# The first pair of seven products prepared during the output projection, and the product that sums the squares placed behind a low pass

## The reference

```python
mixed = jnp.concatenate([o_a, o_b, o_c], axis=-1)   # three attention groups
h = h + mixed @ w_out                               # output projection, 1024 x 1024
f = rms_norm(h, ffn_norm)
gate, up = jnp.split(f @ w_gate_up, 2, axis=-1)     # 1024 x (2 x 2816)
return h + (jax.nn.silu(gate) * up) @ w_down        # 2816 x 1024
```

## Time and profile before

| | us |
|---|---|
| median of three runs | 1295.46 |
| the profiled execution, its own time | 1295.57 |
| its span | 1293.5 |
| PE busy | 1259.0 (97%) |
| DVE busy | 901.5 (70%) |
| ACT busy | 633.9 (49%) |
| POOL busy | 439.4 (34%) |

### The profile page before, as it was taken

How to read it: one execution, slowest core, us unless ns; L and a number is a source line. 1 busy time by engine, 2 the same in 40 slices (tenths; PEclk the granted TensorE clock), 3 DMA queues, 4 the chain that set the end, 5 groups by cost and what they waited for, 6 DMA issues and landing times.

```text
span 1293.5 us, 22962 instructions
## 1 busy us (share of the span) xinstructions
PE 1259.0 (97%) x9174; PEld 1187.0 (92%) x9174; DVE 901.5 (70%) x1520; ACT 633.9 (49%) x1016; POOL 439.4 (34%) x230
## 2 busy tenths in 40 slices
PE   7999999998999999899999999999989999999998
PEld 7989999998999999899998889988779999997887
DVE  4598898488888888722236999984888888885110
ACT  5575556655444444522235665385464445454221
POOL 2563322143222222244445453122432222214543
PEclk9999999999999999999999999999999999999999
DMA  5312211033222231222223221110322332212333
GB/s 189 94 56 83 66 34 34 34 104 115 108 99 99 99 102 63 99 98 98 97 93 101 73 77 55 50 34 24 123 98 98 112 118 99 99 66 98 99 111 115
DMA packets 27440, 113.58 MB, mean 88 GB/s; under 512 B 3664, under 2 KB 4304, under 8 KB 21968
## 3 DMA queue, kind: packets, MB, share of 16 engines
q1 hardware_dynamic: 26624, 111.18, 25.2%
q10 hardware_dynamic: 720, 1.09, 0.2%
HBM read 108.79 MB, written 2.10 MB: 86 GB/s over the span
## 4 chain that ended last, share of the span: by engine, by line
PE 84%; DVE 9%; ACT 3%; issue 2%; DMA 1%; POOL 1%; SPq 0%; DVEq 0%; ACTq 0%; POOLq 0%
PE ps L1243 21%; PE ps L857 17%; PE ps L1249 11%; PE ps L863 8%; PE ps L954 5%; PE ps L960 5%; PE ps L955 5%; PE ps L1084 2%; PE ps L1057 1%; PE ps L1067 1%; PE ps L1032 1%; DVE rstd L2041 1%; DVE score L1866 1%; DMA raw<-in_groups 1%; PE ps L1141 1%
## 5 line engine op out<-in xcount | busy, mean ns | idle before, releaser
L724 POOL TENSOR_TENSOR wlo<-raw,whi 128x1024 fp32r<-128x1024 f32 x116 | 282.9, 2440 | 477.1 <-ACT whi L1327 476.6
L1327 ACT ACTIVATE whi<-raw 128x1024 fp32r<-128x1024 f32 x116 | 122.4, 1057 | 223.8 <-PE ps L863 179.1
L954 PE MATMUL ps<-xhi,whi 128*128 128x264 f32 (+1 forms) x632 | 177.6, 310 | 0.0
L955 PE MATMUL ps<-xlo,whi 128*128 128x264 f32 (+1 forms) x632 | 171.4, 300 | 0.0
L857 PE MATMUL ps<-hhi,whi 128*128 128x264 f32 (+1 forms) x528 | 159.0, 323 | 5.2 <-DVE hlo L2105 5.2
L857 PE MATMUL ps<-hlo,whi 128*128 128x264 f32 (+1 forms) x528 | 159.0, 323 | 0.0
L954 PEld LDWEIGHTS ps<-xhi,whi 128*128 128x128 f32 x632 | 119.1, 189 | 4.5 <-issue 0.4
L955 PEld LDWEIGHTS ps<-xlo,whi 128*128 128x128 f32 x632 | 119.2, 189 | 3.9
L857 PEld LDWEIGHTS ps<-hhi,whi 128*128 128x128 f32 x528 | 100.4, 190 | 13.5 <-DVE hlo L2105 5.8
L857 PEld LDWEIGHTS ps<-hlo,whi 128*128 128x128 f32 x528 | 100.2, 190 | 7.8
L829 POOL TENSOR_TENSOR sums_a<-raw 128x1024 f32<-128x1024 f32 x22 | 53.9, 2449 | 151.4 <-PE ps L1249 151.4
(11 more groups left out here) (275 smaller groups left out, 3337.8 us busy)
## 6 DMA issues: line engine op xcount, KB each, us to landing
raw<-in_weights SPq DMA_DIRECT2D x116, 512.0 KB, 3.3
raw<-in_groups SPq DMA_DIRECT2D x42, 1024.0 KB, 4.8
out_hT<-h SPq DMA_DIRECT2D x7, 256.0 KB, 4.5
h<-in_hT SPq DMA_DIRECT2D x4, 264.0 KB, 6.5
h<-in_hT ACTq DMA_DIRECT2D x4, 264.0 KB, 6.1
cst<-in_consts SPq DMA_DIRECT2D x1, 780.5 KB, 9.4
xnb<-feat SPq DMA_DIRECT2D x20, 33.2 KB, 2.0
feat<-xnb SPq DMA_DIRECT2D x20, 33.2 KB, 2.0
```

The lines of the kernel that those rows point to most:

```text
L724: nc.gpsimd.tensor_tensor(wlo[:, b], raw[:, b], whi[:, b].bitcast(F32), ALU.subtract).then_inc(split_done, 1)
L954: nc.tensor.matmul(o, whi[:, k % 2, n], xhi[:, n, cut], start=(n == 0), stop=False)
L955: nc.tensor.matmul(o, whi[:, k % 2, n], xlo[:, n, cut], start=False, stop=False)
L1327: return nc.scalar.activation(whi[:, b], raw[:, b], ACT.Copy).then_inc(hi_done, 1)
```

## The change

All five engines' programs are edited; what is computed stays.

- SP issues the load of pair 1 (`load_group(1)`) behind that of unit 28, where it stood behind that of unit 33.
- POOL makes pair 1's sums (`pv_sums(1)`) behind the split of unit 29, where they stood behind that of unit 33.
- ACT makes `raw_high(1)` at the end of tile 5's steps and `sums_high(1)` at the end of tile 6's, where both stood behind the last forms and a load of the activation table.
- DVE makes `rt_sums(1)` at the end of tile 5's steps and `raw_low(1)` at the end of tile 6's; the two `sums_low(1, ...)` stand before and behind the last `forms_low`.
- PE makes the ones product between the two low passes of the gate unit.

The core of the diff (the functions moved up with their text unchanged are left out):

```diff
@@ SP
+                for n in range(N_PROJ + 4, U_DN):
+                    load_unit(l * UNITS + n, n % 2)
+                    if n == U_OUT + 4:
+                        load_group(1)
+                for n in range(2, GROUPS_7 + 1):
+                    load_group(n)
@@ POOL
+                for n in range(N_PROJ + 2, U_DN):
+                    split_unit(l * UNITS + n, n % 2)
+                    if n == U_OUT + 5:
+                        pv_sums(1)
+
+                for n in range(2, GROUPS_7 + 1):
+                    pv_sums(n)
@@ PE
-                prenorm(1)
                 for n in range(2):
                     pe.wait_ge(split_done, l * UNITS + (U_GU + n + 3))
                     for hf in range(len(parts)):
                         low_pass(n, n, 2 * n + hf, parts[hf], x_tiles, range(KT), True).then_inc(half_done, 2 // len(parts))
+                    if n == 0:
+                        prenorm(1)
@@ ACT
                     elif m:
                         forms_high(m // 2 - 1)
+                    if m == 5:
+                        raw_high(1)
+                    elif m == 6:
+                        sums_high(1)
...
-                raw_high(1)
-                sums_high(1)
                 for n in range(1, GROUPS_7 + 1):
@@ DVE
                     elif m and m % 2 == 0:
                         forms_low(m // 2 - 1)
+                    if m == 5:
+                        rt_sums(1)
+                    elif m == 6:
+                        raw_low(1)
                 dve.wait_ge(ev.sum_hi, 1)
                 nc.vector.tensor_tensor(sum_parts[:, 1, of], rstd[:, of], sum_parts[:, 0, of].bitcast(F32), ALU.subtract).then_inc(ev.sum_split, 1)
                 forms(PAIRS - 1)
+                sums_low(1, SUM_P, 2)
                 forms_low(PAIRS - 1)
+                sums_low(1, SUM_R, 3)
...
-                rt_sums(1)
-                raw_low(1)
-                sums_low(1, SUM_P, 2)
-                sums_low(1, SUM_R, 3)
                 for n in range(1, GROUPS_7 + 1):
```

More of the change, by code:

```diff
@@ L687, in _, with load_group @@
                     do[step[0]](*step[1:])
-                for n in range(N_PROJ + 4, U_DN):
-                    load_unit(l * UNITS + n, n % 2)
-                for n in range(1, GROUPS_7 + 1):
+                def load_group(n):
                     if n == 1:
@@ L816, in _, with pv_sums @@
                     do[step[0]](*step[1:])
-                for n in range(N_PROJ + 2, U_DN):
-                    split_unit(l * UNITS + n, n % 2)
-                for n in range(1, GROUPS_7 + 1):
+                def pv_sums(n):
                     raw_blocks, _, sums, _, _ = group_slot(n)
@@ L1601, in forms_high, with raw_high, sums_high @@
                     nc.scalar.activation(fhi[:, i, :, 0:width], form_sum[:, :, 0:width], ACT.Copy).then_inc(sv.forms_hi, 1)
+                def raw_high(n):
+                    raw_blocks, hi, _, _, _ = group_slot(n)
+                    act.wait_ge(sv.group_loaded[n % 2], 16 * loads_before(l, n))
+                    if n == 2:
+                        act.wait_ge(half_done, half0 + 2 * (U_GU + 2))
+                    elif n > 2:
+                        act.wait_ge(sv.product_done, len(PRODUCTS) * (g0 + n - 2))
+                    nc.scalar.activation(hi[:, 0:3], raw_blocks[:, RAW_B11:RAW_B12 + 1], ACT.Copy).then_inc(sv.group_hi, 1)
+                def sums_high(n):
+                    _, hi, sums, _, _ = group_slot(n)
+                    act.wait_ge(sv.pv_summed, g0 + n)
+                    nc.scalar.activation(hi[:, 3:5], sums[:, SUM_P:SUM_V + 1], ACT.Copy).then_inc(sv.group_hi, 1)
+                    act.wait_ge(sv.rt_summed, 2 * (g0 + n))
+                    nc.scalar.activation(hi[:, 5:7], sums[:, SUM_R:SUM_T + 1], ACT.Copy).then_inc(sv.group_hi, 1)
                 for m in range(KT):
@@ L1624, in _ @@
                 nc.scalar.preload_act_table_set("silu_and_others")
-                def raw_high(n):
-                    raw_blocks, hi, _, _, _ = group_slot(n)
-                    act.wait_ge(sv.group_loaded[n % 2], 16 * loads_before(l, n))
-                    if n == 2:
-                        act.wait_ge(half_done, half0 + 2 * (U_GU + 2))
-                    elif n > 2:
-                        act.wait_ge(sv.product_done, len(PRODUCTS) * (g0 + n - 2))
-                    nc.scalar.activation(hi[:, 0:3], raw_blocks[:, RAW_B11:RAW_B12 + 1], ACT.Copy).then_inc(sv.group_hi, 1)
-                def sums_high(n):
-                    _, hi, sums, _, _ = group_slot(n)
-                    act.wait_ge(sv.pv_summed, g0 + n)
-                    nc.scalar.activation(hi[:, 3:5], sums[:, SUM_P:SUM_V + 1], ACT.Copy).then_inc(sv.group_hi, 1)
-                    act.wait_ge(sv.rt_summed, 2 * (g0 + n))
-                    nc.scalar.activation(hi[:, 5:7], sums[:, SUM_R:SUM_T + 1], ACT.Copy).then_inc(sv.group_hi, 1)
                 def snapshot(n, product, bank_name, to):
@@ L2030, in forms_low @@
                                             ALU.subtract).then_inc(sv.forms_ready, 1)
[L2032 to L2049, removed]
                 def rt_sums(n):
@@ L2071, in sums_low @@
                                             ALU.subtract).then_inc(sv.group_lo, 1)
+                chain(nc.vector.memset(rstd[:], 0.0))
+                for m in range(KT):
+                    dve.wait_ge(half_done, half0 + 2 * (U_OUT + m + 1))
+                    nc.vector.tensor_tensor(tokens(l, h[:, m]), wide(l, 2 * (m % 2)), tokens(l, h[:, m]), ALU.add).then_inc(ev.acc_free, 1)
+                    dve.wait_ge(ev.acc_free, 2 + m + 1)
+                    x_low(m, par[:, P_FFN + m:P_FFN + m + 1], l * (2 * KT) + (KT + m), of)
+                    dve.wait_ge(ev.sq_ready, len(SQUARES) + m + 1)
+                    if m:
+                        dve.wait_ge(ev.summed, m)
+                    nc.vector.tensor_tensor(rstd[:, of], rstd[:, of], sqb[:, m % 2, of], ALU.add).then_inc(ev.summed, 1)
+                    if m % 2 and m < KT - 1:
+                        forms(m // 2)
+                    elif m and m % 2 == 0:
+                        forms_low(m // 2 - 1)
+                    if m == 5:
+                        rt_sums(1)
+                    elif m == 6:
+                        raw_low(1)
+                dve.wait_ge(ev.sum_hi, 1)
+                nc.vector.tensor_tensor(sum_parts[:, 1, of], rstd[:, of], sum_parts[:, 0, of].bitcast(F32), ALU.subtract).then_inc(ev.sum_split, 1)
+                forms(PAIRS - 1)
+                sums_low(1, SUM_P, 2)
+                forms_low(PAIRS - 1)
+                sums_low(1, SUM_R, 3)
                 def u_sum(n):
```

## The result

The changed kernel takes 1310.2 us (median of four runs, 1308.27 to 1310.94), the kernel before 1295.4 us. The ratio is 1.0114, with a 95% interval of 1.0096 to 1.0131: slower by 14.8 us. The profiled execution took 1309.73 us, with a span of 1307.7 us where before it was 1293.5. The granted clock over the span was 0.992 instead of 0.997.

A forecast was written before the change was run, and what follows sets the result against it. PE, 97% busy, was taken as the bound. Ones product late 4.7 and 5.0, loads 1.0 and clock 2.8 us sum to 13.5 us on 1295.57: 1309.1, or 1309 for the median; range 1302 to 1313.

The forecast's parts named there:

- The chain of 11.1 us: Pair 1's third product starts 11.1 us (layer 1: 11.2) after the ones product, whatever PE does between; the change leaves this.
- The replay of DVE and POOL: Output projection replayed with row durations and port lock: layer 0 `h` adds of tiles 6 and 7 late by 5.4 and 6.0 us.
- The order of the ones product: Ones product behind the first low pass, squares ready in time: +1.2 us in layer 0, -0.2 us in layer 1.
- Ones product late by 4.7 and 5.0 us: Late `h` adds and the low pass ahead delay the ones product 4.7 us in layer 0, 5.0 us in layer 1.
- the second rival: Half-clock spells in the gate products too, after their 2 us wait: 16.3 us slower, 1312; chance 15%.
- The loads, +1.0 us: Pair 3's load right behind pair 2's makes pair 2's land 0.5 us later in each layer, 1.0 us together.
- The clock, 2.8 us in two spells: One half-clock spell per layer in the products after the 3.6 us wait before the third product, 1.4 us each.
- The first rival: No spell of low clock behind the new waits: 9.7 + 1.0 us slower, 1306; chance 22%.
- The third: Projection has room, DVE's lateness absorbed between the adds: 1297.5, within no change; chance 6%.
- the fourth: Faster: third product bound by `hi_a`, `lo_raw_a` and squares, not pair 2's load, so waits go: 1290; chance 3%.

The follow-up runs named there:

- the two runs that moved the rounding: ACT rounds pair 2's blocks behind both snapshots of pair 1: on the changed kernel 1304.8 us, on the kernel before 1296.4 us.
- POOL's sum late: Kernel before, with POOL's pair sum for pair 1 waiting until DVE has made the last forms: 1293.7 us, ratio 0.9985.
- POOL's move alone: Kernel before with only the load of pair 1 and POOL's pair sum moved into the output projection: 1294.7 us, ratio 1.0003.
- the last kernel: Kernel before with POOL's pair sum behind last forms, pair 2's rounding behind snapshots, pair 1's load and ACT block rounding early, lo_raw ahead of DVE's sums: 1288.7 us.
- the kernel with the rounding moved: Kernel before, with ACT rounding pair 2's blocks behind both snapshots of pair 1: 1296.4 us, ratio 1.0003.
- the run with the ones product back: Changed kernel with the ones product ahead of both low passes again, the preparation staying in the output projection: 1306.9 us, ratio 1.0095.

## Why the prediction was right

1309 was forecast, in a range of 1302 to 1313, and 1310.2 was measured. Point by point:

*The chain of 11.1 us* held: 11.1 us in layer 0, 970.36 - 959.40 = 11.0 in layer 1. That it runs over pair 2's load and ACT's order was shown by the two runs that moved the rounding. Where another link of the chain got longer it grew with it, to 11.9 us in layer 1 with POOL's sum late.

*The replay of DVE and POOL* held within 0.1 us in the adds of tiles 6 and 7 of both layers (+5.4, +6.0 and +3.7, +5.4 forecast). The lock costs what the rows said, 2.89 us for a 0.7 us instruction. What it said of PE in layer 0 held too: waits of 1.0 and 2.2 us in the gate unit were forecast and are 0.90 and 2.02. The runs add what it could not say: POOL's move alone is even, and the loss comes with DVE's pieces ahead of the adds.

*The order of the ones product*, +1.2 and -0.2 us on an undisturbed path, was +1.1 and 0.0 when done alone.

*Ones product late by 4.7 and 5.0 us*: 4.8 and 6.6. The term of layer 1 was sized too small; the missing 1.6 us is the half clock in the gate unit, which I had left to the second rival.

*The loads, +1.0 us*: wrong. With the next load right behind it, pair 2's load landed after 4.87 us in layer 0, against 4.77, and after 4.82 in layer 1, against 4.84: 0.1 us and none, not 0.5 in each. The row that I took it from, a 512 KB load ahead of a 1 MB one, did not carry over. The Trainium skill, DMA: Bandwidth & Descriptors, "Queues, rings and completion order", has each DMA engine consume its descriptors in ring order, by which the load behind adds nothing. These landings agree with it.

*The clock, 2.8 us in two spells*: 1.6 + 2.4 us behind the third products and 1.6 in the gate unit of layer 1, 5.6 us in all, twice the term. The spell in layer 1 behind the third product was twice as long as the one in the earlier trace rows, and there was the one in the gate unit. 5.6 us is the clock of the second rival, in other places. The reason given did not hold in layer 0 either: a spell was to follow a wait of 3.6 us, but the wait was 1.79 us, and the spell came all the same. That this half of the term came out near is luck.

So 13.5 us were forecast and 15.3 are found in the stretches, of which the profiled execution gives back 1.1 us by an earlier start. The mechanism is the one forecast, and the closeness of 1309 to 1310.2 is partly luck: the loads came out 0.9 us under their term, the start 1.1 us early, and the clock 2.8 us over. The first rival falls with the spells; the second has the right sum of clock, and its 1312 is missed by what the loads and the start took back. The third, room in the projection, falls with the adds of tile 7, 6 us late; the fourth, with the snapshot's wait that grew instead of going. What I did not see is that a part of the preparation had room: in the last kernel the load and ACT's rounding stand in the projection, and no add of `h` is later than before.

## What to carry to other kernels

Before work is moved into an earlier stage, replay that stage on the engine that gets it, in program order and with the port lock between VectorE and GpSimd, not by its busy share: at 70% busy DVE had no room there, since DVE's new pieces and POOL's lock ahead of the `h` adds, which free PE's banks, made tile 7's add 5 to 6 us late and raised PE's waits for them from 2.2 to 10.3 us. A product that starts a long chain over several engines should go as early as its inputs allow, even where PE has other work that would fill its wait (filling it cost 1.1 us in layer 0 and gained nothing in layer 1). And look for the last link of such a chain: here it was an order of two ACT instructions. Where spells of half clock are worth as much as the edit, compare runs at equal granted clock, too.

## What the runs showed of the hardware

The spells of half clock (1.2 for 2.4 GHz) were worth as much as the edits. The same wait of 3.40 us before the down projection was followed by none (the last kernel), by 3.4 us (the kernel before) and by 6.8 us (the kernel with the rounding moved); waits of 2.0 to 2.2 us in the midst of dense work brought a spell in some places and not in others (none after 301.57 in the changed kernel, one after 302.75 in the run with the ones product back, at nearly the same place in the program). Each 3.4 us cost 1.4 us (12 of 30 products in the earlier trace rows) to 1.6 us (8 of 17 from 951.9) where PE was the path. The clock goes with the time of a run, but it is not all of it. With POOL's sum late, four runs at clock 0.998 took 1290.60 to 1290.97 us and four at 0.996 took 1295.00 to 1295.81; by an estimate 0.002 of a span of 1293 us is 2.6 us, and these lie 4 us and more apart. Where the rest comes from is not shown.

The lock has an order. In layer 0 of the changed kernel DVE's `xlo` came at 273.17 us, during a split, and ended at 275.49, 0.57 us behind it, while the pair sum, which came at 274.88, took 2.85 us instead of some 2.4. The `rstd` sum, which came at 275.41, then waited for the pair sum to end. So a waiting VectorE instruction got its turn between two GpSimd instructions that followed each other, and the waiting GpSimd instruction got in before the next one of VectorE.
